# First mixer of the second block: attention steps of head pairs woven into the projections, bias added in PSUM

## The reference

```python
qa, ka, va, qb, kb, vb = jnp.split(hh @ w_in, EVEN_SPLITS, axis=-1)
qa = rms_norm(qa.reshape(bsz, n, A_HEADS, HEAD_DIM), a_qn)      # also ka, qb, kb: 26 heads of norms
...
qa = rope_2d(qa, row, col); ka = rope_2d(ka, row, col)          # latent tokens only
# A:  s = q k^T * scale + window mask;  softmax over [keys, sink];  o = p v
# B:  s = q k^T * scale + bias, masked; softmax over keys;          o = p v
y_lat = jnp.concatenate([o_a, o_b], axis=-1) @ w_out
y_ctx = jnp.concatenate([oa_c, ob_c], axis=-1) @ w_out
```

## Time and profile before

| what | us |
|---|---|
| median of 3 runs | 2629.16 (2628.22 to 2632.52) |
| profiled execution, its own time | 2625.06 |
| its span in the trace | 2623.4 |
| busy PE / DVE / ACT | 2340.9 / 1578.5 / 830.6 |
| granted clock of PE, mean | 0.918 |
| this mixer (1273.57 to 1641.37) | 367.80 |

### The profile page before, as it was taken

The page is one execution under the profiler, slowest core; times in us unless marked ns, Lnnn a source line. Parts: engine busy times, 40 slices in busy tenths (PEclk is TensorE's granted clock), DMA queues, the critical chain, the costliest instruction groups (busy, mean ns, idle before and its releaser), DMA issues.

```text
span 2623.4 us, 39655 instructions
## 1 busy us (share of the span) xinstructions
PE 2340.9 (89%) x14932; PEld 1943.1 (74%) x14932; DVE 1578.5 (60%) x2834; ACT 830.6 (32%) x1274; POOL 29.0 (1%) x58
## 2 busy tenths in 40 slices
PE   8999579999999888999696999599999568797999
PEld 7999448999999877998582557478878453166987
DVE  6666667666666657665535884662552565556764
ACT  4444324444444544443010452011111010153332
POOL 0000000000000000000000000000000000000000
PEclk9999859999999988999896899799999787599999
DMA  7656204665665423666120002022222110001444
GB/s 249 240 208 218 81 0 154 238 213 199 241 230 184 154 97 125 237 221 236 68 96 0 1 1 85 32 96 96 96 96 96 48 65 16 0 1 65 160 169 151
DMA packets 50221, 325.66 MB, mean 124 GB/s; under 512 B 5328, under 2 KB 8656, under 8 KB 16976
## 3 DMA queue, kind: packets, MB, share of 16 engines
q1 hardware_dynamic: 42480, 266.61, 28.9%
q0 software_dynamic: 7648, 57.81, 6.0%
HBM read 323.35 MB, written 1.05 MB: 124 GB/s over the span
## 4 chain that ended last, share of the span: by engine, by line
PE 80%; DVE 14%; ACT 3%; issue 2%; DMA 0%; DVEq 0%; ACTq 0%; PEldq 0%; SPq 0%
PE psum L1319 17%; PE psum L1320 16%; PE psum L1321 16%; PE psum L1406 3%; PE psum L1444 3%; PE psum L1473 3%; PE psum L1407 3%; PE psum L1408 3%; PE psum L1491 3%; PE psum L1465 3%; PE psum L1701 2%; PE psum L1423 2%; PE psum L1480 1%; DVE w_lo L627 1%; PE psum L1702 1%
## 5 line engine op out<-in xcount | busy, mean ns | idle before, releaser
L1319 PE MATMUL psum<-h_hi,w_hi 128*128 128x256 f32 (+2 forms) x2568 | 796.7, 310 | 115.9 <-DVE h_lo L815 84.7
L393 ACT ACTIVATE w_hi<-raw 128x1024 fp32r<-128x1024 f32 (+1 forms) x542 | 513.6, 990 | 859.1 <-PE psum L1321 648.8
L1320 PE MATMUL psum<-h_lo,w_hi 128*128 128x256 f32 (+2 forms) x2568 | 785.1, 306 | 0.0
L1321 PE MATMUL psum<-h_hi,w_lo 128*128 128x256 f32 (+2 forms) x2568 | 784.6, 306 | 0.0
L627 DVE TENSOR_TENSOR w_lo<-raw,w_hi 128x1024 fp32r<-128x1024 f32 (+1 forms) x542 | 599.8, 1148 | 230.9 <-ACT w_hi L393 211.1
L1319 PEld LDWEIGHTS psum<-h_hi,w_hi 128*128 128x128 f32 (+1 forms) x2568 | 496.2, 193 | 162.7 <-issue 64.8
L1321 PEld LDWEIGHTS psum<-h_hi,w_lo 128*128 128x128 f32 (+1 forms) x2568 | 495.9, 193 | 19.4
L1320 PEld LDWEIGHTS psum<-h_lo,w_hi 128*128 128x128 f32 (+1 forms) x2568 | 496.1, 193 | 18.9
L1406 PE MATMUL psum<-g_both,w_hi 128*128 128x256 f32 x704 | 202.4, 287 | 2.1 <-DVE w_lo L627 2.1
L1407 PE MATMUL psum<-g_both,w_hi 128*128 128x256 f32 x704 | 199.1, 283 | 0.0
L1408 PE MATMUL psum<-g_both,w_lo 128*128 128x256 f32 x704 | 199.1, 283 | 0.0
(11 more groups left out here) (231 smaller groups left out, 2888.6 us busy)
## 6 DMA issues: line engine op xcount, KB each, us to landing
raw<-in_weights SPq DMA_DIRECT2D x207, 1024.0 KB, 4.9
raw_ada<-in_ada POOLq DMA_DIRECT2D x48, 1024.0 KB, 6.8
raw<-in_weights SPq DMA_DIRECT2D x64, 704.0 KB, 4.1
arena<-in_rpb POOLq DMA_DIRECT2D x1, 2048.0 KB, 9.7
arena<-in_fox_c POOLq DMA_DIRECT2D x1, 1888.0 KB, 8.7
const_region<-in_even_c POOLq DMA_DIRECT2D x1, 1360.0 KB, 8.8
const_region<-in_latent_c POOLq DMA_DIRECT2D x1, 1296.0 KB, 6.2
x_res<-in_x_lat SPq DMA_DIRECT2D x4, 256.0 KB, 6.9
```

The source lines that it names most:

```text
L393: nc.scalar.activation(wh[s][:, a], raw[s][:, a], ACT.Copy).then_inc(hi_ready, 1)
L1319: mm(out, sh, mh, start=n == 0, stop=False)
L1320: mm(out, sh, ml, start=False, stop=False)
L1321: ins = mm(out, sl, mh, start=False, stop=n == len(pairs) - 1)
```

## The change

The mixer becomes one stream of items that all engines walk in one order (`even_order`): a projection unit, sums of squares one chunk behind, `root`, `spread`, `rope` when their inputs are there, from unit 8 on one or two `slot`s behind a unit, then slots with output units, then the last output units. A slot is one stage of a software pipeline of 24 steps. A step is a pair of heads: 16 steps have 128 latent queries with 512 keys, 8 have 2 x 128 context queries with 256 keys. The two heads of a pair lie in the upper and lower 64 partitions of one chunk; the columns of `e_w_in` and the rows of `e_w_out` for attention A are reordered on the host so that heads c and c+4 pair up, and the copies of the key heads go. The scale is folded into the query gains, mask and bias are added in PSUM by a product with the identity, the maximum is taken straight from PSUM for both heads, POOL adds the column mask, ACT takes the squares. The output projection runs as two halves over the inner dimension (16 units of 12 products): A's while B's steps run. In stick the preload of the table with exp and log moves behind the first square root.

```diff
+        def even_order():
+            slots = iter(range(len(E_STEPS) + 3))
+            for n in range(18):
+                yield "unit", n
+                if 1 <= n <= 5 or 7 <= n <= 14:
+                    yield "sum", n - 1 - (n > 6)
+                if n == 5:
+                    yield "root", 0
+                if n == 6:
+                    for c in range(5):
+                        yield "spread", c
+                if n == 7:
+                    for c in range(5):
+                        yield "rope", c
+                if n == 14:
+                    yield "root", 1
+                if n in (15, 16):
+                    for c in range(4):
+                        yield "spread", 5 + 4 * (n - 15) + c
+                if n >= 8:
+                    for _ in range(1 + (n in (12, 16))):
+                        yield "slot", next(slots)
+            for k in slots:
+                yield "slot", k
+                if 15 <= k <= 22:
+                    yield "out", k - 15
+            for q in range(8, 16):
+                yield "out", q
...
# POOL
+                nc.gpsimd.tensor_tensor(b_bias[:, t, :, :], b_bias[:, t, :, :],
+                                        col_mask.unsqueeze(1).broadcast_to([P, 8, T]), ALU.add).then_inc(e_bias_ready, 1)
...
# ACT, slot k
+                    act.wait_ge(st_shifted, k + 1)
+                    if s["kind"] == "a":
+                        nc.scalar.activation(st_small[:, 32 + z:32 + z + nj], st_small[:, 24 + z:24 + z + nj], ACT.Exp)
+                    for n, (m, t, col) in enumerate(s["jobs"]):
+                        nc.scalar.activation(st_p[:, 2 * (k % 2) + m, col:col + s["L"]], psum[:, 2 + m, col:col + s["L"]],
+                                             ACT.Exp, bias=st_small[:, z + n:z + n + 1],
+                                             accum_out=st_small[:, 8 + z + n:9 + z + n]).then_inc(st_exp, 1)
+                if 1 <= k <= len(E_STEPS):
+                    act.wait_ge(st_turned, k)
+                    wait(act, st_out, k - 2)
+                    for m in range(2):
+                        nc.scalar.activation(st_pt[:, 2 * ((k - 1) % 2) + m, :], psum[:, 4 + m, :],
+                                             ACT.Copy).then_inc(st_turn_in, 1)
...
# ACT, stick
-                    nc.scalar.preload_act_table_set("natural_log_exp_and_others")
                     for what, k in stick_order():
                         if what == "proj":
                             stage(1, 1, 1, 1, lead=(lambda: square_one(7)) if k == (0, 0) else None)
+                            if k == (0, 0):
+                                nc.scalar.preload_act_table_set("natural_log_exp_and_others")
...
# DVE
+            def step_shift(k):
+                dve.wait_ge(st_scored, k + 1)
+                if nj == 4:
+                    step(V.reduce_max(mx.rearrange("p (a b) -> p a b", a=2), src.rearrange("p a (b c) -> p a b c", b=2), AX_X))
+                else:
+                    step(V.reduce_max(mx, src, AX_X))
+                if s["kind"] == "a":
...
+            def step_weigh(k):
+                dve.wait_ge(st_exp, sum(len(v["jobs"]) for v in E_STEPS[0:k + 1]))
+                if s["kind"] == "a":
+                    step(V.tensor_tensor(tot, tot, es, ALU.add))
+                step(V.reciprocal(rec, tot))
+                for n, (m, t, col) in enumerate(s["jobs"]):
+                    p = st_p[:, 2 * (k % 2) + m, col:col + s["L"]]
+                    ins = V.tensor_scalar(p, p, rec[:, n:n + 1], None, ALU.mult)
+                ins.then_inc(st_prob, 1)
...
+                    elif what == "slot":
+                        if k < len(E_STEPS):
+                            step_shift(k)
+                        if k >= 3:
+                            step_read(k - 3)
+                        if 1 <= k <= len(E_STEPS):
+                            step_weigh(k - 1)
...
# PE
+            def step_scores(k):
+                wait(pe, st_exp, sum(len(v["jobs"]) for v in E_STEPS[0:k]))
...
+                        ins = mm(psum[:, 2 + m, col:col + L], e_qk[r, q, base + t * P:base + (t + 1) * P],
+                                 e_qk[r, key, TJ - L:TJ], start=True, stop=base != 0)
+                if base == 0:
+                    for m, t, col in s["jobs"]:
+                        bias = w_mask[:, t, :] if s["kind"] == "a" else b_bias[:, t, 2 * c + m, :]
+                        ins = mm(psum[:, 2 + m, 0:T], ident, bias, start=False, stop=True)
+                ins.then_inc(st_scored, 1)
+            def step_turn(k):
+                pe.wait_ge(st_prob, k + 1)
...
+                    elif what == "slot":
...
+                        if k < len(E_STEPS):
+                            step_scores(k)
+                        if 1 <= k <= len(E_STEPS):
+                            step_turn(k - 1)
+                        if 2 <= k <= len(E_STEPS) + 1:
+                            step_out(k - 2)
```

More of the change, by code:

```diff
@@ new lines, in even_steps @@
+        def even_steps():
+            steps = []
+            for kind in "ab":
+                for c in range(4):
+                    group = 8 * (kind == "b") + 2 * c
+                    for t in range(2):
+                        steps.append(dict(kind=kind, c=c, base=0, L=TJ, jobs=[(m, t, 0) for m in range(2)],
+                                          group=group, first=t == 0, last=t == 1))
+                    steps.append(dict(kind=kind, c=c, base=T, L=T, jobs=[(m, t, t * T) for m in range(2) for t in range(2)],
+                                      group=group + 1, first=True, last=True))
+            return steps
@@ L422, in square_root @@
                 act.wait_ge(n_summed, pos.n("root", 1))
-                nc.scalar.activation(n_root[:], psum[:, 7, 0:T], ACT.Sqrt, bias=small[:, 40:41]).then_inc(n_rooted, 1)
+                nc.scalar.activation(n_root, psum[:, 7, 0:T], ACT.Sqrt, bias=small[:, 40:41]).then_inc(n_rooted, 1)
             def stage(n, per_iter, ev, units, extra=None, peel=0, last=False, w=SLOT, lead=None):
@@ new lines, in even @@
+            def even():
+                sums = 0
+                unit_of = {}
+                for what, k in even_order():
+                    if what == "unit":
+                        if k % 2 == 0:
+                            hi_next(0, 0, 1, pos.e, SLOT)
+                            pos.p += 1
+                        unit_of[k] = pos.u
+                        pos.u += 1
+                        pos.e += 1
+                    elif what == "sum":
+                        act.wait_ge(bank_free, unit_of[k + (k >= 5)] + 3)
+                        wait(act, e_sq_used, sums - 1)
+                        nc.scalar.activation(e_sq[:, sums % 2, :], e_qk[:, k, :], ACT.Square).then_inc(e_sq_made, 1)
+                        sums += 1
+                    elif what == "root":
+                        rows = (10, 16)[k]
+                        act.wait_ge(e_sq_used, (5, 13)[k])
+                        nc.scalar.activation(e_row[0:rows, :], psum[0:rows, 7, :], ACT.Sqrt,
+                                             bias=small[0:rows, 40:41]).then_inc(e_rooted, 1)
+                    elif what in ("spread", "rope"):
+                        pos.u += 1
+                        pos.e += 1
+                    elif what == "slot":
+                        step_slot(k)
+                    else:
+                        if k % 4 == 0:
+                            hi_next(0, 0, 1, pos.e, SLOT)
+                            pos.p += 1
+                        pos.u += 1
+                        pos.e += 1
@@ L562, in _ @@
             norm(TJ)
[L563 to L567 removed]
+            even()
             norm(TJ)
@@ L1647, in joint_chunks @@
                             ).then_inc(gemm_done, 1)
+            def step_scores(k):
+                s = E_STEPS[k]
+                c, L, base = s["c"], s["L"], s["base"]
+                wait(pe, st_exp, sum(len(v["jobs"]) for v in E_STEPS[0:k]))
+                q, key = (c, 4) if s["kind"] == "a" else (5 + c, 9 + c)
+                for t in sorted({job[1] for job in s["jobs"]}):
+                    for m in range(2):
+                        r = slice(64 * m, 64 * m + 64)
+                        col = 0 if base == 0 else t * T
+                        ins = mm(psum[:, 2 + m, col:col + L], e_qk[r, q, base + t * P:base + (t + 1) * P],
[5 more added lines that the diff above has]
+                ins.then_inc(st_scored, 1)
```

291 lines of the change are left out of this document (194 added, 97 removed).

## The result

| what | before | after |
|---|---|---|
| median of 6 runs each, us | 2629.9 (2628.22 to 2632.52) | 2648.32 (2638.16 to 2651.22) |
| profiled execution, us | 2625.06 | 2650.23 |
| mean granted clock | 0.918 | 0.911 |
| this mixer in the trace, us | 367.80 | 406.55 |

The changed kernel is slower: ratio 1.0063, 95% interval 1.0045 to 1.0081, +18.4 us in the medians. Cut at the same work on PE, the difference is: up to the end of stick -23.2, from there to the mixer +5.8, the mixer +38.75, behind it +3.6. Together +25.0.

The account below looks back on a forecast made before the run. PE was taken as the bound: its work, waits and clock. Mixer -1 at full clock, clock +56, stick -25 gave +30 on 2625.06, so 2655; the runs' median stands 4.1 higher, so 2659 us, range 2600 to 2705.

Parts of the forecast that it names:

- The slot waits: Mixer slots: PE stands from the end of scores through DVE's whole row, 2.8 to 4.1 us each, some 84 us.
- Other waits: Mixer outside those 84 us: three slots at the end 5, rotation 4.8, second reciprocal 3.4, first spread 1.8, output 1.
- PE's work: Mixer: projection 106, sums 12.0, spreads 11.7, slots 93 where the jobs had 154, output 44 us at full clock.
- Spreads: Mixer's head norms: 13 spreads, now at the full clock, about 0.9 us each, 11.7 us.
- The clock: Mixer: PE's waits drop its clock, 2.0 us per slot for 25 slots, plus 6 for two units: 56 us.
- the 0.7 to 0.8 that I gave as its sign: Mixer slots: granted clock expected in the trace after if waits drop PE's clock.
- The first rival: Every slot: PE's clock holds through the waits, so the 56 us fall away, time 2603 us; chance 0.22.
- Clock stays down in the last slots: Last twelve slots, no projection unit following: clock stays at 0.5, +44 us, time 2703 us; chance 0.13.
- Stick: Stick mixer: moved preload removes table loads among the pairs, 17.7 us of waits and 7.5 of clock: -25 us.
- The mask at 0: Column mask moved to GpSimd, done long before step 12 needs it: 0 us, bounds 0 to 7.

Follow-up runs that it names:

- the second maximum: Changed kernel with DVE's maximum over 1024 columns taken twice in each slot, second result unread: 2684.86 us, ratio 1.0212.
- weighing first: Changed kernel with DVE in each slot weighing step k-1 before reading step k-3 and taking the maximum of step k: 2567.8 us, ratio 0.9769.
- the filled wait: Changed kernel with useless PE products in each slot between scores and the wait for the weighing: six 2613.89 us, three 2626.13 us.
- the mask later: Changed kernel with GpSimd's column-mask addition held until the mixer's first projection unit is done: 2643.45 us, ratio 1.0062; also combined with other edits.

## Why the prediction came out as it did

The forecast, 2659 us, is 10.7 above the median, on the right side and by its main mechanism. In the profiled executions it stood at +30 against +25.2. That is closer than its terms are, and so far it is luck: the mixer was put 16 us too high (422.7 against 406.55: idle 16.6 and clock 4.3 too high, work 4.8 too low), and 9.4 us elsewhere were not foreseen (+5.8 and +3.6).

- **The slot waits: right.** 84 us predicted for 20-odd waits of 2.8 to 4.1, measured 78.2 in 23, most of them 2.8 to 3.8. One is 5.54, with the second reciprocal (3.34) in it. More DVE work in the row came out one for one as waiting (the second maximum), and less of it ahead of the weighing as less (weighing first).
- **Other waits: 16 us foreseen, 5 found.** I had 5 for the three slots at the end, 4.8 for rotation, 3.4 for the reciprocal on its own, 1.8 for the first spread and 1 at the output, in all 100 with the 84. The trace has 1.5 for rotation, 0.4 for the first spread and none in the slots behind the last transposes; total idle 83.4.
- **PE's work: right.** 266.7 at the full clock by the terms, 271.5 measured. Pairs of scores and of values do overlap: L1823 1.13 us for 4 records, the same as one head in the earlier trace rows within 0.08; values 1.09 for 16 records, where eight took 1.02. Spreads were 0.9 predicted, but the ten records of five took 6.1 us, 1.2 each, since they still ran partly at half the clock; the other eight took 8.1, 1.0 each.
- **The clock: right in kind, 56 predicted, 51.7 measured.** 44.2 in 23 slots is 1.9 per slot against the 2.0 taken. The mean granted clock of the slots, 0.81 to 0.84, is above the 0.7 to 0.8 that I gave as its sign, in part because the idles themselves count as full clock in it; over PE's busy time alone it is 0.80 (44.2 of 223.5 us lost). The first rival (the clock holds) is out with the 44.2 us lost; the filled wait shows that they hang on PE's idle. The page "TensorE: Matmul & The Clock Gate" of the Trainium skill (Loop structure matters more than you think) has a DVE copy out of PSUM that doesn't break PE's warmth in a loop where the next products follow immediately. I had read 0 from it for this case, which was wrong: here the next products wait 3.4 us for DVE, so the measurement doesn't contradict that sentence.
- **Clock stays down in the last slots: out.** 0.84 and 0.81 in the first and the last slots' windows, where this rival had 0.50 in the last twelve; in the slot shown it came back within 4 us.
- **Stick: -25 predicted, -23.2 measured**, of it 17.9 idle (17.7 predicted) and 8.9 clock (7.5). Against these 26.8 stand 3.6 us more of PE's work at the full clock between the same marks. The page "ScalarE: Activation LUTs" (What ACT_TABLE_LOAD costs) with its 2.66 us a switch led to -29; the two runs with the preload moved say -23.7 and +23.5.
- **The mask at 0: a term put at nothing that was not.** It costs 3 us ahead of the mixer, within the bounds of 0 to 7, but not by a path I named: I counted DVE's products that go, and not that GpSimd's 8.96 us fall on a product of DVE on the path. The Trainium skill states the rule, in "SBUF — State Buffer" (SBUF: two separate sides): a DVE operation with two inputs in SBUF and a GpSimd operation that reads SBUF share a pair of ports by an exclusive lock, held for the whole instruction. The trace agrees: the reciprocal, with one input, keeps its 3.35 us beside GpSimd, while the product with two ends 0.7 us after GpSimd does.
- **Not settled: 2.8 of the 5.8 us ahead of the mixer and the 3.6 behind it.** No run was made for them, but the kept traces speak for chance. With the preload alone, and so with the old mixer, the mixer begins at 1254.1 us, no sooner than in the versions with the mask later (1251.1 to 1253.9). From the first product of the next projection to the end it takes 951.0 us after, against 947.0 before and 948.7 with the preload alone, and 949.6 to 952.4 in all but one of the other versions. That one, the changed kernel with the preload put back, takes 947.9, and its loss to half clock there is that of before (61.9 against 62.2 us; 65.6 after). So the new mixer doesn't force the 3.6.

Where the gain went, then: the new mixer takes 39.7 us of work off PE. Its idle, nearly all of it the wait for one DVE row per slot, took 52.5 back and the clock 26.0 more. With one line order changed on DVE the same mixer is 37 us faster than the old one (2567.8 against 2604.88, both with the preload moved).

## What to carry to other kernels

When two pipelines are woven together, write down for each wait of the busiest engine which instructions stand ahead of the releasing one on the other engine; the piece that the busiest engine waits for goes first in that row, and a piece that frees a buffer goes before the one that only feeds later work. Price such a wait with its clock: here 78 us of idle cost another 44. Before spending on a rewrite, test the clock's share with useless products in the wait, and test single lines of a large change alone: one line of this one, the preload, was worth 23.7 us.

## What was not expected of the hardware

- Short idles cost clock too, but not each of them. In the mean 3.4, 1.9 and 0.7 us of idle per slot lost 1.9, 0.9 and 0.1 us; one idle of 2.07 us cost and one of 2.98 didn't. In the profile of before the one idle of 1.83 us had lost nothing, from which I had expected such idles to cost little.
- Useless work on TensorE made the kernel faster by 34 us.
- GpSimd stretched a pair of DVE operations with two inputs in SBUF from 0.88 to 3.84 us (the norm's products), and another pair from 2.36 to 4.88 (the low halves of a panel).
